# Sample states' decay as eight scalar operations behind the product with z, and cache copies two weight chunks earlier, in a hybrid decoder step

## The reference, cut to what matters

```
s = jnp.exp(cum[:, -1])[..., None, None] * s + jnp.einsum('bsgh,bsghp,bsgn->bghpn', to_end, xc, bc)
y = y + d_skip[:, :, None] * xs.astype(jnp.float32)
y = gated_group_rmsnorm(y.reshape(b, l, D_INNER).astype(x.dtype), z, p['ssd_norm'])
```

## Time and profile before

| | |
|---|---|
| median of 3 runs | 2932.91 us (2931.29 to 2938.15) |
| the profiled execution | 2932.58 us |
| its span, first to last instruction | 2930.9 us |
| mean granted TensorE clock | 0.983 |
| PE busy | 2808.0 us (96%) |
| DVE busy | 1392.7 us (48%) |
| ACT, POOL busy | 826.3 us (28%), 835.8 us (29%) |
| moved by DMA | 303.04 MB, mean 103 GB/s |

### The profile page before, as it was taken

One profiled execution on the slowest core, in us unless ns is written; L12 is line 12 of the kernel. 1 busy time (PEld: TensorE's weight loads), 2 busy tenths in 40 slices (PEclk: granted clock), 3 DMA queues, 4 the chain that ended last, 5 costly groups with the idle time before them and its releaser, 6 DMA issues.

```text
span 2930.9 us, 46443 instructions
## 1 busy us (share of the span) xinstructions
PE 2808.0 (96%) x17725; PEld 2624.9 (90%) x17725; DVE 1392.7 (48%) x2390; ACT 826.3 (28%) x1977; POOL 835.8 (29%) x554
## 2 busy tenths in 40 slices
PE   7999999999999999999999976889999999999997
PEld 5989998999999899999999963359999999999997
DVE  5485557647565762212323236677733333333334
ACT  4463155126414511333332332213410000000004
POOL 2342334324422434112121100024042323232332
PEclk9999999999999999999999988989999999999999
DMA  5545335344534532122231356973011111111111
GB/s 176 174 123 159 105 118 172 103 144 121 175 93 129 164 111 97 32 73 61 60 81 45 82 159 186 292 235 119 23 51 44 49 39 51 37 51 37 51 48 66
DMA packets 334137, 303.04 MB, mean 103 GB/s; under 512 B 26320, under 2 KB 302336, under 8 KB 332328
## 3 DMA queue, kind: packets, MB, share of 16 engines
q1 hardware_dynamic: 249464, 243.09, 27.1%
q10 hardware_dynamic: 84456, 56.93, 6.5%
HBM read 250.81 MB, written 102.91 MB: 121 GB/s over the span
## 4 chain that ended last, share of the span: by engine, by line
PE 89%; DVE 3%; DMA 3%; issue 2%; ACT 1%; POOL 1%; SPq 0%; ACTq 0%; DVEq 0%; POOLq 0%
PE ps L2173 24%; PE ps L2174 24%; PE ps L2175 24%; PE ps L2464 2%; PE ps L2443 2%; PE ps L2334 1%; PE ps L2330 1%; PE ps L2455 1%; PE ps L2548 1%; PE ps L2333 1%; PE ps L2532 1%; PE ps L2589 1%; DMA wraw<-in_w_out_dram 1%; DMA smqrep<-q_scr 1%; PE ps L2383 1%
## 5 line engine op out<-in xcount | busy, mean ns | idle before, releaser
L2173 PE MATMUL ps<-hH,wH 128*128 128x352 f32 (+1 forms) x2208 | 739.0, 335 | 8.7 <-issue 4.5
L2175 PE MATMUL ps<-hH,wL 128*128 128x352 f32 (+1 forms) x2208 | 722.4, 327 | 0.0
L2174 PE MATMUL ps<-hL,wH 128*128 128x352 f32 (+1 forms) x2208 | 722.2, 327 | 0.0
L775 POOL CAST wH<-wraw 128x1024 fp32r<-128x1024 f32 (+1 forms) x178 | 195.8, 1100 | 1550.3 <-PE ps L2175 1230.5
L777 POOL TENSOR_TENSOR wL<-wraw,wH 128x1024 fp32r<-128x1024 f32 (+1 forms) x178 | 443.6, 2492 | 14.3
L2173 PEld LDWEIGHTS ps<-hH,wH 128*128 128x128 f32 x2208 | 416.7, 189 | 33.8 <-issue 26.5
L2174 PEld LDWEIGHTS ps<-hL,wH 128*128 128x128 f32 x2208 | 417.2, 189 | 0.4
L2175 PEld LDWEIGHTS ps<-hH,wL 128*128 128x128 f32 x2208 | 416.1, 188 | 0.0
L2173 PE MATMUL ps<-mH,wH 128*128 128x384 f32 (+1 forms) x1128 | 371.4, 329 | 2.7 <-issue 2.7
L2174 PE MATMUL ps<-mL,wH 128*128 128x384 f32 (+1 forms) x1128 | 371.1, 329 | 1.0 <-issue 0.8
L2175 PE MATMUL ps<-mH,wL 128*128 128x384 f32 (+1 forms) x1128 | 370.1, 328 | 0.0
(11 more groups left out here) (405 smaller groups left out, 4664.2 us busy)
## 6 DMA issues: line engine op xcount, KB each, us to landing
wraw<-in_w_in_dram SPq DMA_DIRECT2D x92, 512.0 KB, 3.9
wraw<-in_w_up_dram SPq DMA_DIRECT2D x44, 512.0 KB, 3.7
ssdcr<-cum_scr ACTq DMA_DIRECT2D x32, 512.0 KB, 4.5
out_dram<-in_cache_kv_w_dram SPq DMA_DIRECT2D x16, 960.0 KB, 5.5
smkraw<-in_cache_kv_w_dram SPq DMA_DIRECT2D x45, 256.0 KB, 7.1
wraw<-in_w_down_dram SPq DMA_DIRECT2D x22, 512.0 KB, 3.6
smkraw<-in_cache_kv_w_dram SPq DMA_DIRECT2D x9, 1024.0 KB, 6.4
smvraw<-in_cache_kv_w_dram SPq DMA_DIRECT2D x35, 256.0 KB
```

The source lines that it names most:

```text
L775: pool.tensor_copy(hi, a).then_inc(w_hi, 1)
L2173: pe.matmul(dst, hi, cols(mH[:, k, :], c), start=k == 0, stop=False)
L2174: pe.matmul(dst, hi, cols(mL[:, k, :], c), start=False, stop=False)
L2175: last = pe.matmul(dst, lo, cols(mH[:, k, :], c), start=False, stop=k == kt - 1)
```

## The change

The multiplication of a head pair's states by their decays, one tensor operation over 128 x 1024 with the decay broadcast along 128 columns, is taken out. Behind the product of y and z stand eight operations instead, one for each sequence: 128 x 128 elements times a scalar for each partition, read from the tile "small". The last of them raises `s0_new`. In SP's program the copies are issued behind chunks 2 to 15 of a group, not 4 to 17, with the same parts in the same order; behind chunk 3 the copy comes ahead of the waits and of the parameter loads. (Counted from 1 within the group, these are chunks 3 to 16 and 5 to 18.)

```
@@ -686,8 +686,8 @@
                     for k, (src, kt, w) in enumerate(chunks(i)):
                         load(i * per + (first + k), src, kt, w, first + k)
-                        if stage == 1 and k >= 4:
-                            copy_part(i * 2 + (k - 4) // 7, (k - 4) % 7)
+                        if stage == 1 and 2 <= k < 16:
+                            copy_part(i * 2 + (k - 2) // 7, (k - 2) % 7)
                         if stage == 1 and k == 3:
@@ -1677,12 +1677,13 @@
                     s = s0[hp % 2]
                     dve.wait_ge(s0_tr, g * 4 + hp + 1)
                     dve.tensor_copy(s0t[:, 0:4, :].rearrange("p b n -> p (b n)"), A[1][:, :]).then_inc(s0t_dve, 1)
-                    dve.tensor_tensor(s[:, :, :], s[:, :, :], eclg[:, hp, :].unsqueeze(2).to_broadcast([P, DB, P]),
-                                      ALU.mult).then_inc(s0_new, 1)
                     if hp == 0:
                         dve.wait_ge(yev_done, g * NCH + NT)
                     dve.wait_ge(zs_silu, g * XT + hp + 1)
                     dve.tensor_tensor(xs[:, hp, 0:SEQ], xs[:, hp, 0:SEQ], zs[:, hp, 0:SEQ], ALU.mult).then_inc(gate_done, 1)
+                    for b in range(DB):
+                        ins = dve.tensor_scalar(s[:, b, :], s[:, b, :], ecd[:, hp, b:b + 1], None, ALU.mult)
+                    ins.then_inc(s0_new, 1)
                     dve.wait_ge(s0_new, g * 12 + 3 * hp + 1)
                     dve.wait_ge(s0_up, g * 4 + hp + 1)
```

## The result

The change makes the kernel slower: 2943.21 us in the median of 5 runs (2939.46 to 2948.59) against 2932.91, a ratio of 1.0034 with a 95% interval from 1.0018 to 1.0049. The prediction was 2932.9 us within 2928 to 2938, and "the same" (within 0.2%) with 0.86; the time lies outside the range, 10 us above the forecast. The profiled execution took 2939.46 us, 6.9 more than the one before. In the code after, the lines of PE's products and of DVE's adds are one higher (L2174 for L2173, L1692 for L1691).

The account below looks back on a forecast made before the run. PE (TensorE) was taken as the bound, busy 96% of the span. The profiled 2932.58 us + 0 (decay) + 0 (copies) = 2932.6; with 0.3 for the median of the runs, 2932.9 us, range 2928 to 2938.

Parts of the forecast that it names:

- part two: SP's copies, issued two chunks earlier in each group: no wait of PE moves, 0 us, bounds 0 and +0.
- that maximum as a bound for SP alone: Parameter loads behind copy 3 on SP: 3.47 us issue plus 10.1 gives 330.3 at worst, before DVE's need at 332.38.
- Part one, the decay: DVE's state work: eight scalar operations behind the product replace one multiplication; DVE done 0.8 us later, PE unaffected, 0 us.
- inherited the stall: DVE, head pair 1: the product with z takes over the multiplication's wait for POOL, 3.24 us, ending at 233.37.
- The eight: DVE's scalar decay operations behind the product with z: 1.9 us together, between 1.5 and 2.2.
- DVE's idle time before the adds: DVE's wait for PE's update product, as a sign: down from 5.2 to about 4.4 us.
- POOL's last addition: End of POOL's chain in the state part, as a sign: still about 1 us ahead of PE's sums matmul.
- 1 (POOL kept out before the sums): DVE's last scalar operations delay POOL's final addition, 1.7 us late in each of 4 groups: 6.8 us, 2939.7; chance 0.05.
- 2 (parameters late): Parameters come late behind copy 3 on SP, costing PE 2 to 3 us in 3 groups: 2939 to 2942; chance 0.03.
- 3 (the standstills move): PE's standstills at the groups' start become alike, 4.4 us either way: 2928.5 or 2937.3; chance 0.08.
- 4 (both standstills go): Both of PE's standstills at the groups' start vanish, 6.2 us faster: 2926.7; chance 0.04.
- a sign of being wrong: On PE: a wait for ysum, conv's evictions or a split, or a group-start standstill of another length, would disprove the forecast.

Follow-up runs that it names:

- (3): The changed kernel with the order of the copy parts turned, so chunks 4 to 15 carry the same parts as in the kernel before: 2932.31 us, 0.9997.
- (4): The kernel before with only the order of the copy parts turned by two, a full 1 MB part behind chunk 10: 2937.00 us, 1.0015.
- (7): The changed kernel with the 1 MB part behind chunk 10 issued as two transfers of 512 KB: 2934.53 us, 1.0004.
- after_wide: The changed kernel with the decay as one 128x1024 operation behind the product with z, not eight: 2941.45 us, 1.0020.

## Why the prediction was wrong

**The step that failed** is in part two: "From chunk 4 on a copy stands behind each load as before, only its content is another." The content mattered. Behind chunk 10 one transfer took the place of two, and 3.6 us later ACT issues its small stores. With it fell "Sum of part two: 0 us, bounds 0 and +0": it should have held 4 x 1.2 to 2.0 us, 5.7 in the profiled execution. Shown by undoing it (3), by doing it alone (4) and by splitting it (7).

The profile of before held the warning. In the earlier trace rows an issue of a copy takes 0.54 us in the median and 3.47 at most, and I used that maximum as a bound for SP alone. The same bound on ACT's three stores would have put 3 us in front of an eviction with 1.3 us of cover: (3.0 - 1.3) x 4 = 7 us, or about 2940: nearer to the 2943.21, though still 3 short. (The 1.3 us are read from the trace after; before the run they would have been an estimate.) ACT's own queue had a warning as well, among its loads of `ssdcr` in the kernel before:

```profile
L1052 ACTq DMA_DIRECT2D ssdcr<-cum_scr x36: 379/380/1422, 75.7 to 980.7; - x36
```

I named the queues that the copies were moved past (SP's), not those that issue while a copy moves.

**Part one, the decay: right.** DVE's timeline in head pairs 0 and 1 of group 0, after, for the earlier trace rows:

```profile
219.98 1.23 DVE L1683 TENSOR_TENSOR xs<-xs,zs 128x1024 f32<-128x1024 f32 x1 [0.47 <-ACT zs L1146]
221.13 3.81 DVE L1685 TENSOR_SCALAR ssds<-ssds,small 128x128 f32<-128x128 f32 x8
...
234.41 3.24 DVE L1683 TENSOR_TENSOR xs<-xs,zs 128x1024 f32<-128x1024 f32 x1
237.58 1.65 DVE L1685 TENSOR_SCALAR ssds<-ssds,small 128x128 f32<-128x128 f32 x8
243.96 1.28 DVE L1692 TENSOR_TENSOR ssds<-ssds,ps 128x512 f32<-128x512 f32 x2 [4.74 <-PE ps L2384]
```

- In head pair 1 the product inherited the stall, 3.24 us as forecast. With the wide form of the decay behind it (after_wide) it is 3.24 too and the decay 1.21, so there the stall belongs to whichever comes first.
- The eight take 1.65 us, 0.21 each (forecast 1.9, bounds 1.5 to 2.2). DVE's idle time before the adds is 4.74 us (forecast 4.4): 5.18 less 1.65 - 1.21.
- In head pair 0 the product got through and the eight were held, 3.81 us; POOL's subtraction there:

```profile
220.11 3.37 POOL L777 TENSOR_TENSOR wL<-wraw,wH 128x1024 fp32r<-128x1024 f32 x1
```

It ends at 223.48, and the eight end 1.46 us later, the time of some seven of them. So operations with a single source in SBUF are kept out by POOL too. This agrees with the rule of the Trainium skill ("SBUF — State Buffer", separate sides of SBUF) that such an operation in a two-port mode takes the shared lock; the trace doesn't show in which mode they ran. The estimate of 1.0 us for the eight by the figures of the Trainium skill ("VectorE: DVE Perf Modes", TRN2 errata) was too low against the measured 1.65.
- POOL's last addition still ends 1.0 us ahead of the sums matmul (272.65 against 273.68), for the earlier trace rows:

```profile
270.26 2.39 POOL L836 TENSOR_TENSOR ysum<-ysum,ysq 128x1024 f32<-128x1024 f32 x1 [3.77 <-ACT ysq L1158]
```

```profile
273.68 1.50 PE L2360 MATMUL ps<-ysum,ones 128*128 128x384 f32 x4
```

**Part two, the new places: right for PE, off in how late the parameters are.** SP's queue at the end of group 0, for the earlier trace rows:

```profile
309.07 0.58 SPq L540 DMA_DIRECT2D out_dram<-in_cache_kv_w_dram  x1
...
320.96 0.54 SPq L540 DMA_DIRECT2D out_dram<-in_cache_kv_w_dram  x1
321.88 0.35 SPq L696 DMA_DIRECT2D ccg<-cc_scr  x1
```

PE is 4.28 us later than before in this stretch (273.68 against 269.40). The parameter load is 5.14 later, so 0.9 late (forecast 0.5 to 0.7), and lands in 4.8 us, not 3.1. The ones behind it are later still, because one of them (tokg) takes longer to issue, 1.42 us where it took 0.33 before; the last two start at 325.21 in place of 318.87, 2.1 us late, which the forecast of 0.5 to 0.7 for each didn't have:

```profile
323.60 1.42 SPq L700 DMA_DIRECT2D tokg<-tok_scr  x1
325.21 1.50 SPq L704 DMA_DIRECT2D small<-cl_scr  x2
```

DVE needs the first at 336.81, 4.43 later than in the earlier trace rows, and the idle time behind that is still there:

```profile
336.81 0.17 DVE L1570 COPY small<-nrm 128x4 f32 x1 [4.42 <-issue]
...
340.60 0.65 DVE L1596 COPY ncg<-ssdc 128x3 f32<-128x3 f32 x1 [3.19 <-ACT ssdc L949]
```

**The rivals.** 1 (POOL kept out before the sums) and 2 (parameters late) didn't happen. 3 (the standstills move) did, but not by the change: PE's entry "issue" for 75 to 1130 us sums to 4.5 and 4.0 us in two executions of the kernel before and to 1.7, 3.9 and 2.1 in three of the changed one. So a standstill of another length, which I had named as a sign of being wrong, was no sign. One execution against another can differ by 4.1 us for that alone. 4 (both standstills go) didn't happen either: none of these sums is below 1.7. The mechanism that did happen wasn't among them; of the 0.09 that I gave to slower, 0.08 lay with DVE, POOL and SP and 0.01 with PE's standstills, none with ACT's queue.

**What stays open.** Why a second transfer on SP's queue, even of 16 KB, frees the first issue on ACT's queue; no run tells. ACT's 512 KB load right ahead of the stores isn't the reason, at least not by being late itself: in group 1 it lands in 6.9 us in the changed kernel, 5.8 before, and in 7.4 with 960 + 64 KB, where the first store is issued in 0.4. And a remainder: 6.8 us of time against 4.9 us of waits or 5.9 by start times (10.3 against 5.7 or 6.6 for the first measurement alone). The scatter between measurements, some 0.0025 or 7 us for one program, is enough for it. Part of it can be placed: between the same two products of PE, at about 1719 and 1953 us, behind all that was changed, the 20 profiled executions took 231.0 to 240.0 us, and two of the kernel before 233.8 and 238.2. Whether a second effect hides in the remainder wasn't settled.

## What to carry to other kernels

When transfers move along a queue, list what stands where afterwards by size and number of transfers, and look in the trace for every engine that issues a DMA of its own while they are under way (here 3.6 us behind them): the issue occupied ACT, and behind it stood its evictions. Take the longest issue that the trace shows as the bound for every issue that gets a new neighbour, and compare it with the cover of what follows. And a profiled execution of each kernel is one draw: a standstill of 1 to 4 us that has no releaser is compared over several before it is put down to a change.

## What the runs showed of the hardware

- ACT's issue of a small store (13.5 KB), 0.38 us elsewhere, takes 1.6 to 3.3 us when one copy of 960 or 1024 KB from memory to memory, issued 3.6 us earlier on SP's queue, is under way. With a second transfer of 16, 64 or 512 KB right behind the copy the first store's issue is 0.38 to 0.39 us in the median; with 512 KB the second store's is then 1.4.
- A copy of 1 MB goes out as sixteen packets of 64 KB. Behind chunk 10 of the changed kernel each takes 2.4 to 3.9 us, 2.5 in the median of group 1. In two halves they are 32 packets of 32 KB with 1.2 us at the least and 2.7 at most, 1.25 in the median of group 1.
- Eight scalar operations of 128x128 take 1.65 us on DVE where one two-operand operation of 128x1024 takes 1.21, and beside a POOL subtraction of 3.37 us the eight took 3.81 us, and the one, as the wide decay behind the product in after_wide, 3.43.
